# RWKV-7 group norm split into early and late columns with one variance row per head, gate and bonus computed earlier, state decay on VectorE and the sample state steps inside the solve levels

## The chip, the cores and the metric

The kernel runs on one core of one Trainium2 chip. The metric is the device time of one execution in microseconds (us). All arithmetic is float32. Besides TensorE (PE) with its weight load (PEld), the core has VectorE (DVE), ScalarE (ACT), GpSimd (POOL) and SyncE (SP), which issues most of the DMAs.

## The reference

One inference step of a two-layer decoder for 256 prompt tokens and 8 sample tokens (264 columns together). Each layer is a half-step FFN, a mixer (8 RWKV-7 heads beside 8 MLA heads), a cross-attention into 256 memory tokens, and a second half-step FFN. The change lies wholly in the mixer, and there in the RWKV half:

```
def step(S, inp):
    r_t, w_t, k_t, v_t, kk_t, b_t = inp
    S_kk = jnp.einsum('bhvk,bhk->bhv', S, kk_t)
    S = S * w_t[:, :, None, :] - S_kk[..., None] * b_t[:, :, None, :] + v_t[..., None] * k_t[:, :, None, :]
    return S, jnp.einsum('bhvk,bhk->bhv', S, r_t)
...
g = jax.nn.sigmoid(gd) @ g_up
mean = jnp.mean(o, axis=-1, keepdims=True)
var = jnp.mean(jnp.square(o - mean), axis=-1, keepdims=True)
o = ((o - mean) * lax.rsqrt(var + GN_EPS)).reshape(B, T, W) * gn_w + gn_b
bonus = jnp.sum(r_h * k_h * r_k, axis=-1, keepdims=True) * v_h
out = (o + bonus.reshape(B, T, W)) * g
...
x = x + jnp.concatenate([o_rwkv, o_mla], axis=-1) @ w_out[l]
```

The mean and the variance are taken per head and token over 64 values.

## The kernel before, in words

Activations lie transposed: features on the 128 partitions, the 264 tokens in the free dimension. Each engine has its own program, written by hand in the order in which it runs; a loop goes over the two layers. The engines meet through semaphores (`signal(name).by(...)` counts one up, `.at(k)` is the value that a wait wants). Every DVE and ACT instruction waits for the one before it on its engine.

The RWKV part of a layer stands between the MLA attention and the output projection, and has four stages.

1. **Operands** (`rwkv`, `solve` on PE). From the decays, four products per token are made: AR (kk and r), Bt, Kt, and their pairwise products MB and MK in 64-token chunks, two chunks (one pair `T`) to 128 partitions.
2. **Solve levels.** The inverse of a unit triangular 64x64 matrix per head and chunk is built in LEVELS = 6 doublings, so five rounds n = 1 to 5. In each round PE multiplies Y = Ml X for T = 0, 1, ACT copies Y out of PSUM, PE multiplies XT Y and Y XT, and DVE subtracts the results from X and XT (four 128x512 `TENSOR_TENSOR` a round; the last round has only the two of XT). GpSimd prepares the masks of the next rounds (`keep_level`, L509). `between(n)` puts further PE work between the two halves of a round. Behind the four subtractions DVE does one `step_samples(n - 1)` (a 128x2048 instruction of the 8 sample tokens' state update, nine of them numbered 0 to 8) and one `dcm` (the decay matrix of a chunk).
3. **Chunks** (`chunks` on PE). For the chunks n = 0 to 3 in turn: u = WT Z (64 rows, 4 products), DVE copies U out; PE adds into bank 6 the new keys (tok 2 times tok 3), the old state (identity times Z) and tok 1 times U, and DVE multiplies by the decay (`dcm[n]`) into Z[n + 1]. PE computes chunk n - 1's outputs before it waits for chunk n's U. Two `keep_warm` products (128x264, result unused) stand ahead of each wait for Z. DVE does `step_samples(5 to 8)` behind the first two U copies.
4. **Group norm, bonus, gate** (end of `rwkv` on PE and DVE). Over all 264 columns and 4 tiles: sums per head by the 128x128 matrix `blk`, subtraction of the mean, squares on ACT, sums of the squares (each on 64 partitions at once), a `RECIPROCAL` over 128x1056, a square root, and three further DVE instructions a tile, with the r k r_k product, the bonus and the gate in between.

Then `mix_out` multiplies by W_out in 8 column tiles, each in two halves of four products: half 0 takes the MLA rows, half 1 the RWKV rows. The first half of tiles 0 to 3 is issued as soon as the gate is out of PSUM; half 1 of each tile waits for `rwkv_mixed`. The weights come in 1 MB blocks of two tiles through a ring of two slots (`ring_c`): the block of tiles 4 and 5 is requested by SP when the two tiles of the first block are through. GpSimd's DMA queue loads the sample tokens' memory keys 4 to 7 (4 MB) after the last state and the last outputs, and the prompt memory (1 MB) after `rwkv_mixed`.

## Time and profile before

| | us |
|---|---|
| median of 3 runs (1904.67 to 1909.27) | 1905.67 |
| the profiled execution | 1913.24 |
| its span, first to last instruction | 1911.7 |
| PE busy | 1788.4 (94%) |
| PEld busy | 1483.9 (78%) |
| DVE busy | 638.0 (33%) |
| ACT busy | 315.1 (16%) |
| POOL busy | 84.5 (4%) |

The mean granted TensorE clock is 0.971 of full speed. One product in float32 stands as two instructions in the records, so a count of x32 is 16 products. Times in the traces are from the start of the span. The RWKV part of the first layer lies at 427 to 544 us, that of the second at 1363 to 1479 us.

### The profile page before, as it was taken

The numbers are of one execution on the slowest core, as the hardware profiler recorded it, in microseconds if no ns is written. First come the engines' busy times: TensorE is split into PE (matmuls) and PEld (weight loads), VectorE is DVE, ScalarE is ACT, GpSimd is POOL, SyncE is SP. The second block draws the span as 40 slices with busy tenths as digits, with TensorE's granted clock in tenths as the row PEclk, the third lists the DMA queues.
The fourth block names the chain that finished last, engine by engine and source line by source line (L and its number), as shares of the span: only waits on it lengthen the run. The fifth ranks groups of instructions, "written<-read, shape, count | busy, mean of one in ns | idle before, by whom it ended". The sixth has DMA issues, their size and how long they took to land.

```text
span 1911.7 us, 30695 instructions
## 1 busy us (share of the span) xinstructions
PE 1788.4 (94%) x11846; PEld 1483.9 (78%) x11846; DVE 638.0 (33%) x1250; ACT 315.1 (16%) x617; POOL 84.5 (4%) x99
## 2 busy tenths in 40 slices
PE   6999999878889999999999999997798999999995
PEld 5888887558767888888888888874686878888884
DVE  3111136548563321111121112546585612311122
ACT  1111002432100311110011100134221013111100
POOL 0000000014000000000000000000320000000000
PEclk9999999989899999999999999999799999999998
DMA  5444543841246634443434455346303474344431
GB/s 202 146 141 176 196 165 109 221 136 47 103 169 218 219 137 160 143 154 146 162 133 138 147 205 201 127 143 188 117 27 138 172 272 150 130 137 151 170 125 78
DMA packets 70641, 291.58 MB, mean 153 GB/s; under 512 B 8209, under 2 KB 41170, under 8 KB 41730
## 3 DMA queue, kind: packets, MB, share of 16 engines
q1 hardware_dynamic: 63938, 246.57, 37.7%
q0 software_dynamic: 6448, 42.20, 6.0%
q8 instruction: 70, 1.15, 0.3%
q10 hardware_dynamic: 144, 1.32, 0.2%
q14 instruction: 41, 0.34, 0.1%
HBM read 281.47 MB, written 8.59 MB: 152 GB/s over the span
## 4 chain that ended last, share of the span: by engine, by line
PE 86%; DVE 9%; ACT 2%; issue 2%; DMA 1%; DVEq 0%; SPq 0%; POOL 0%; ACTq 0%; POOLq 0%
PE bank L366 81%; DVE arena L1450 3%; PE bank L878 3%; PE bank L369 2%; ACT arena L1206 1%; DVE ring_a L1450 1%; DVE arena L1487 1%; DVE arena L1465 1%; DMA ring_c<-in_blocks 1%; DVE hT L1459 0%; DVE arena L1462 0%; DVE sq L1450 0%; DVE sq L1621 0%; DVE hT L1450 0%; DVE arena L1454 0%
## 5 line engine op out<-in xcount | busy, mean ns | idle before, releaser
L366 PE MATMUL bank<-hT,ring_a 128*128 128x264 f32 x2816 | 629.5, 387 | 18.9 <-DVEq L97 18.7
L366 PEld LDWEIGHTS bank<-hT,ring_a 128*128 128x128 f32 x2816 | 535.9, 190 | 111.1 <-issue 19.3
L366 PE MATMUL bank<-arena,ring_b 128*128 128x264 f32 x1408 | 314.3, 386 | 5.1 <-DVE arena L1514 5.1
L366 PEld LDWEIGHTS bank<-arena,ring_b 128*128 128x128 f32 x1408 | 267.2, 190 | 52.3 <-issue 6.8
L366 PE MATMUL bank<-arena 64*64 64x64 f32 (+6 forms) x3568 | 190.4, 273 | 20.8 <-DVE arena L1450 11.8
L366 PE MATMUL bank<-hT,ring_c 128*128 128x264 f32 x832 | 195.4, 393 | 12.5 <-DVE hT L1450 5.8
L366 PEld LDWEIGHTS bank<-hT,ring_c 128*128 128x128 f32 x832 | 158.8, 193 | 46.9 <-issue 8.4
L366 PEld LDWEIGHTS bank<-arena 64*64 64x64 f32 (+3 forms) x3568 | 149.1, 135 | 55.2 <-issue 44.4
L366 PE MATMUL bank<-arena,ring_c 128*128 128x264 f32 (+1 forms) x768 | 174.0, 385 | 1.3 <-ACT arena L1206 1.3
L366 PEld LDWEIGHTS bank<-arena,ring_c 128*128 128x128 f32 x768 | 144.9, 190 | 28.5 <-issue 5.0
L1206 ACT ACTIVATE arena<-bank 128x512 f32<-128x512 f32 (+5 forms) x220 | 95.4, 434 | 304.8 <-PE bank L366 255.6
L1514 DVE TENSOR_TENSOR arena<-arena,bank 128x264 f32 x88 | 37.8, 429 | 280.6 <-PE bank L366 276.3
L1510 DVE TENSOR_TENSOR arena<-bank,rstd 128x264 f32<-128x264 f32 x88 | 38.1, 433 | 247.6 <-PE bank L366 242.7
L1225 ACT ACTIVATE arena<-arena 128x264 f32<-128x264 f32 x88 | 37.2, 422 | 493.7 <-DVE arena L1510 493.7
L1459 DVE SCALAR_TENSOR_TENSOR sq<-bank,rstd 128x264 f32<-128x264 f32 x32 | 13.8, 433 | 253.7 <-PE bank L366 253.7
L1206 ACT ACTIVATE rstd<-rstd 128x264 f32<-128x264 f32 x9 | 3.8, 423 | 504.6 <-DVE rstd L1487 504.6
L366 PE MATMUL bank<-ring_c,arena 128*128 128x256 f32 (+2 forms) x472 | 72.5, 371 | 0.8 <-DVE arena L1462 0.8
L369 PE MATMUL bank<-con,arena 128*128 128x128 f32 (+1 forms) x284 | 43.7, 294 | 25.7 <-ACT arena L1206 25.7
L366 PEld LDWEIGHTS bank<-ring_c,arena 128*128 128x128 f32 (+1 forms) x472 | 55.5, 150 | 15.0 <-issue 8.2
L369 PEld LDWEIGHTS bank<-con,arena 128*128 128x128 f32 (+1 forms) x284 | 34.2, 148 | 35.1 <-issue 32.6
L878 PE MATMUL bank<-arena 64*64 64x64 f32 (+3 forms) x608 | 51.9, 268 | 6.7 <-DVE arena L1450 6.7
L1225 ACT ACT_TABLE_LOAD x44 | 56.5, 1283 | 1.7 <-ACT rstd L1206 1.0
(143 smaller groups left out, 1084.5 us busy)
## 6 DMA issues: line engine op xcount, KB each, us to landing
ring_a<-in_ffn_gu SPq DMA_DIRECT2D x88, 1024.0 KB, 4.8
ring_c<-in_blocks SPq DMA_DIRECT2D x58, 1024.0 KB, 4.9
ring_b<-in_ffn_down SPq DMA_DIRECT2D x32, 1408.0 KB, 6.2
arena<-in_pages SPq DMA_DIRECT2D x128, 144.0 KB, 2.5
arena<-in_mem_k POOLq DMA_DIRECT2D x8, 1024.0 KB, 7.8
arena<-in_mem_v POOLq DMA_DIRECT2D x8, 1024.0 KB, 7.2
ring_c<-in_pages SPq DMA_DIRECT2D x48, 144.0 KB, 2.5
ring_a<-in_pages SPq DMA_DIRECT2D x48, 144.0 KB, 2.4
```

Of the source, the lines that this page charges most:

```text
L366: return nc.tensor.matmul(out, lhsT, rhs, start=start, stop=stop)
L369: return nc.tensor.transpose(out, in_, ident[0:n, 0:n])
L878: return nc.tensor.matmul(out, lhsT, rhs, start=start, stop=stop, skip_group_check=True)
L1206: chain(nc.scalar.activation(out, in_, func, **more), signal(done) if done else None)
L1225: nc.scalar.activation(silu[:, u, :], silu[:, u, :], ACT.Silu), KF // 2)
L1450: chain(nc.vector.tensor_tensor(out, a, b, op), out_of(done))
L1459: chain(nc.vector.scalar_tensor_tensor(out=out, in0=a, scalar=s, in1=b, op0=op0, op1=op1), out_of(done))
L1465: chain(nc.vector.tensor_reduce(out, a, AX.X, ALU.max), out_of(done))
L1487: chain(nc.vector.reciprocal(ap, ap), signal("inverse_ready"))
L1510: nc.vector.tensor_tensor(silu[:, u, :], bank[u][:, 0:NT], rstd[:], ALU.mult), KF // 2)
L1514: nc.vector.tensor_tensor(hidden[:, 2 * i + u, :], silu[:, u, :], bank[2 + u][:, 0:NT], ALU.mult), KF // 2)
```

## The change

The order on DVE, in a layer's RWKV part, from the fourth solve round's last subtraction to the second chunk's U copy (register instructions left out). `bank` is PSUM; `ring_a<-...` 128x2048 are the sample steps, `arena<-con,arena` 128x512 is a `dcm`.

Before:

```order
L1450 TENSOR_TENSOR arena<-arena,bank5 128x512 [waits xt_ready,x_out]
L1450 TENSOR_TENSOR ring_a<-sq,ring_b 128x2048 [waits xt_out]
...
L1450 TENSOR_TENSOR arena<-con,arena 128x512 [waits dve_step]
...
L1450 TENSOR_TENSOR arena<-arena,bank2 128x512 [waits xt_ready,dve_step]
L1450 TENSOR_TENSOR arena<-arena,bank5 128x512 [waits xt_ready,xt_out]
L1450 TENSOR_TENSOR ring_a<-ring_a 128x2048 [waits xt_out]
...
L1462 COPY arena<-bank0 64x512 [waits wt_ready,dve_step]
L1450 TENSOR_TENSOR ring_a<-sq,ring_b 128x2048 [waits u_out]
...
L1450 TENSOR_TENSOR ring_a<-ring_a 128x2048 [waits dve_step]
...
L1450 TENSOR_TENSOR arena<-bank6,arena 128x512 [waits tok_turned,z_ready,vector_milestones]
L1462 COPY arena<-bank0 64x512 [waits u_ready,z_out]
```

The change:

```order
L1502 TENSOR_TENSOR ring_a<-ring_a 128x2048 [waits xt_out]
...
L1502 TENSOR_TENSOR ring_a<-ring_a,ring_b 128x2048 [waits vector_milestones]
...
L1502 TENSOR_TENSOR arena<-con,arena 128x512 [waits dve_step]
...
L1502 TENSOR_TENSOR small<-bank6,arena 128x264 [waits tensor_milestones,scalar_milestones]
...
L1511 SCALAR_TENSOR_TENSOR small<-small,vec,ring_b 128x264 [waits vector_milestones]
...
L1506 TENSOR_SCALAR ring_b<-ring_b,vec 128x264 [waits dve_step]
...
L1502 TENSOR_TENSOR arena<-arena,bank2 128x512 [waits xt_ready,dve_step]
L1502 TENSOR_TENSOR arena<-arena,bank5 128x512 [waits xt_ready,xt_out]
L1520 TENSOR_REDUCE sq<-ring_a 128x32 [waits xt_out]
...
L1514 COPY arena<-bank0 64x512 [waits wt_ready,dve_step]
L1502 TENSOR_TENSOR arena<-bank6,arena 128x512 [waits tok_turned,z_ready,u_out]
L1514 COPY arena<-bank0 64x512 [waits u_ready,z_out]
```

All nine steps now stand in the rounds (two in each of rounds 1 to 4, one in round 5), none between the chunks; rounds 4 and 5 also hold the bonus instructions (`small`, three a tile, two tiles a round; one tile stands here of each four).

On PE the second and third chunk. Before:

```order
L366 MATMUL bank<-con,ones 128x264 x2
L379 REGISTER_ALU [waits z_out]
L379 REGISTER_ALU [waits wt_out]
L878 MATMUL bank<-arena 64x128 x4
L878 MATMUL bank<-arena 128x128 x4
L878 MATMUL bank<-arena,con 128x128 x4
L878 MATMUL bank<-arena 64x64 x16
L379 REGISTER_ALU [waits u_out]
L878 MATMUL bank<-arena 128x128 x4
```

The change:

```order
L380 REGISTER_ALU [waits z_out]
L380 REGISTER_ALU [waits wt_out]
L859 MATMUL bank<-arena 64x128 x4
L859 MATMUL bank<-arena 128x128 x4
L380 REGISTER_ALU [waits u_out]
L859 MATMUL bank<-arena 128x128 x4
L859 MATMUL bank<-arena 128x64 x4
L859 MATMUL bank<-arena 64x64 x16
```

The two unused products and the identity product are gone, and a chunk's outputs (128x64 and 64x64) stand behind its own state product instead of ahead of it.

The rest of the change in the code: the tiles' places; the gate product on PE in the attention, in place of four unused products; the bonus products in `between`; PE behind the chunk loop, whose body for n < 3 now issues keys, state and outputs of its own chunk; and DVE's rounds and chunks.

```diff
+EARLY = 3 * CHUNK
-        r = Region(arena, MIX, ARENA)
-        gate = r.take(NJ, NT)
-        bonus = r.take(NJ, NT)
-        e1 = r.take(NJ, NT)
-        e2 = r.take(NJ, NT)
+        gate, bonus = w1, small[:, 0:NJ * NT].rearrange("p (j t) -> p j t", j=NJ)
+        r8 = wstat[0:H, :]
...
-                keep_warm(4, 6)
+                pe.wait_ge(*signal("prob_t_out").at(units))
+                pe.wait_ge(*signal("olat_out").at(units))
+                pe.wait_ge(*signal("gd_ready").at(1))
+                for j in range(NJ):
+                    last = mm(bank[2 * j + 1 if j < 3 else 6][:, 0:NT], sw("g_up")[:, j * P:j * P + P], p[:, 13, :])
+                signal("gate_up").by(last)
...
                 def between(n):
+                    if n >= 4:
+                        wait_apart(pe, signal("rkr_ready").at(1))
+                        for i in range(2):
+                            if n == 5:
+                                wait_apart(pe, signal("bonus_out").at(i + 1))
+                            else:
+                                wait_apart(pe, signal("tok_out").at(9 + i))
+                            signal("bonus_ready").by(mm(bank[6 + i][:, 0:NT], c("blk"), bonus[:, 2 * (n - 4) + i, :]))
...
+                wait_apart(pe, signal("rwkv_out").at(3))
+                centred(False)
+                wait_apart(pe, signal("so_loaded").at(1))
...
+                wait_apart(pe, signal("u_out").at(4))
                 outputs(3)
+                variance(False)
+                wait_apart(pe, signal("rwkv_out").at(4))
+                wait_apart(pe, signal("so_out").at(1))
+                centred(True)
+                new_keys(3)
+                wait_apart(pe, signal("gn_scaled").at(1))
+                variance(True)
+                state(3)
+                spread(False)
+                spread(True)
...
-                    step_samples(n - 1)
+                    for i in range(2 * n - 2, min(2 * n, 9)):
+                        step_samples(i)
...
+                    if n >= 4:
+                        bonuses(n)
...
-                    if n < 2:
-                        step_samples(5 + 2 * n)
-                        step_samples(6 + 2 * n)
+                    if n:
+                        tt(Zd, Z[n], flat(dcm[n]), ALU.mult)
+                    if n == 3:
+                        group_norm()
...
-                    tt(Z[n + 1], bank[6][:, 0:512], flat(dcm[n]), ALU.mult, "z_out")
+                    tt(Z[n + 1], bank[6][:, 0:512], flat(dcm[n]), ALU.mult, None if n else "z_out")
+                    if n:
+                        tt(Z[n + 1], Z[n + 1], Zd, ALU.add, "z_out")
```

`centred` multiplies by one constant matrix that subtracts the head's mean (identity minus 1/64 in the head's block); `variance` sums the squares with an 8-column matrix, one row per head; `spread` brings the eight rows of inverse roots back to 128 partitions. Each runs once for the early columns (0 to 191, chunks 0 to 2) and once for the late (192 to 263). DVE's `group_norm` (behind the fourth U copy) copies the sample outputs, scales the centred values by the gate times gn_w, and takes the reciprocals on 8x192 and 8x72; ACT takes squares (2 of 128x384, 1 of 128x288) and the roots. After the last state DVE multiplies by the spread roots and adds the bonus: two 128x384 products and one 128x768 sum for the early columns, one product and one sum of 128x288 for the late. The bonus tile is now (bonus + gn_b) times the gate. The product r k r_k moves to the end of the attention on DVE; the gate's sigmoid on ACT moves to the projections, its four copies to the time before the MLA outputs, and the sqrt table is asked for ahead of the chunk outputs. In `mix_out`, tile 2 waits for the last state and tile 3 for the early half of `rwkv_mixed`, since the spread roots lie in their banks. The constants grow by 672 columns (344 KB).

## Rows read from the trace of the kernel before

**Rows 1.** Page, part 4: the chain that ended last, by engine.
```profile
PE 86%; DVE 9%; ACT 2%; issue 2%; DMA 1%; DVEq 0%; SPq 0%; POOL 0%; ACTq 0%; POOLq 0%
```
**Rows 2.** Windows, first layer: span, then busy of PE, PEld, DVE, ACT, POOL, clock, DMA.
```profile
451.71:459.41 7.70, 7.70 (x238) 7.46 (x236) 6.67 (x6) 2.40 (x4) 3.91 (x2) 1.00 0.02 4
459.41:465.94 6.53, 6.53 (x230) 6.53 (x228) 5.73 (x6) 2.39 (x4) 3.61 (x3) 1.00 0.01 3
...
473.53:480.91 7.38, 6.10 (x187) 5.83 (x185) 7.10 (x9) 1.19 (x2) 1.09 (x1) 1.00 0.01 2
480.91:489.29 8.38, 5.78 (x137) 4.97 (x133) 8.24 (x5) 1.54 (x4) 0.05 (x1) 1.00 0.02 4
489.29:500.25 10.96, 10.73 (x66) 9.54 (x67) 5.97 (x5) 0.38 (x1) 1.11 (x2) 0.50 0.42 153
500.25:509.30 9.05, 9.05 (x79) 7.47 (x78) 1.37 (x2) 0.38 (x1) 0.53 (x1) 0.85 0.41 168
509.30:516.60 7.30, 7.30 (x82) 6.55 (x80) 1.37 (x2) 0.38 (x1) 0.00 (x0) 1.00 0.01 2
516.60:543.93 27.33, 20.22 (x114) 14.89 (x113) 20.56 (x32) 7.51 (x12) 2.71 (x5) 1.00 0.41 164
543.93:548.20 4.27, 4.27 (x12) 3.42 (x13) 1.93 (x5) 0.00 (x0) 0.53 (x1) 0.60 0.59 182
```
**Rows 3.** Timeline of DVE in rounds 1 and 2: start, duration, engine, line, operation.
```profile
455.41 2.29 DVE L1450 TENSOR_TENSOR ring_a<-ring_a,ring_b 128x2048 f32<-128x2048 f32 x1 [0.22 <-DVE arena L1450]
457.74 1.64 DVE L1450 TENSOR_TENSOR arena<-con,arena 128x512 f32<-128x512 f32 x1
459.41 2.85 DVE L1450 TENSOR_TENSOR arena<-arena,bank 128x512 f32<-128x512 f32 x4
462.30 2.29 DVE L1468 TENSOR_REDUCE sq<-ring_a 128x32 f32<-128x2048 f32 x1
```
**Rows 4.** Timeline of POOL in the same rounds.
```profile
455.50 5.02 POOL L509 TENSOR_TENSOR arena<-arena,con 128x512 f32<-128x512 f32 x2 [4.27 <-PE bank L366]
462.26 2.51 POOL L509 TENSOR_TENSOR arena<-arena,con 128x512 f32<-128x512 f32 x2 [1.75 <-PE bank L366]
```
**Rows 5.** Timeline of PE in the chunks, at the low clock and at the full one.
```profile
489.52 3.94 PE L878 MATMUL bank<-arena 128*64 128x128 f32 x16 [2.03 <-DVE arena L1450]
...
499.35 2.13 PE L366 MATMUL bank<-con,ones 128*128 128x264 f32 x4
...
509.51 2.17 PE L878 MATMUL bank<-arena 128*64 128x128 f32 x16
...
512.60 5.38 PE L878 MATMUL bank<-arena 128*128 128x64 f32 x88
```
**Rows 6.** Timeline of POOL, ACT, DVE and PE in the last chunks and the norm.
```profile
503.41 0.53 POOL L527 DMA_DIRECT2D sq<-sample_outputs  x1 [5.37 <-DMA sample_outputs<-sq]
...
524.68 1.08 ACT L1206 ACTIVATE arena<-hT 128x1056 f32<-128x1056 f32 x1 [4.49 <-PE bank L366]
...
529.84 6.75 DVE L1487 RECIPROCAL arena<-arena 128x1056 f32<-128x1056 f32 x1
...
531.54 7.38 PE L366 MATMUL bank<-hT,ring_c 128*128 128x264 f32 x32 [1.82 <-ACT arena L1206]
```
**Rows 7.** The chain that ended last, at the output projection: start, duration, what.
```profile
543.93 4.19 PE bank L366 x10
...
548.28 4.70 DMA ring_c<-in_blocks
...
553.01 12.06 PE bank L366 x53
```
**Rows 8.** Page, part 6: DMA issues, size of one, median us to landing.
```profile
ring_c<-in_blocks SPq DMA_DIRECT2D x58, 1024.0 KB, 4.9
...
arena<-in_mem_k POOLq DMA_DIRECT2D x8, 1024.0 KB, 7.8
```
**Rows 9.** Timeline of DVE at the start of the RWKV part.
```profile
427.19 1.42 DVE L1450 TENSOR_TENSOR arena<-ring_b 128x512 f32<-128x512 f32 x2 [4.48 <-ACT hT L1206]
```

231 lines of the change are left out of this document (139 added, 92 removed).

## The prediction, made before the changed kernel ran

> **What bounds the kernel now.** I read the page first, then the chain that ended last, then windows over the RWKV part, then timelines. The chain gives PE 86% of the span and DVE 9% [rows 1]: nearly everywhere PE works without a stop, and time can only be won where it doesn't. The change touches one such place in each layer. In the windows of the first layer [rows 2] I cut it at its hand-overs. Solve rounds 1 and 2 take 7.70 and 6.53 us with PE busy throughout. From 473.53 us on DVE is the full engine (7.10 of 7.38, then 8.24 of 8.38 us) until the first chunk state is out at 489.29. Then three chunk rounds of 10.96, 9.05 and 7.30 us go on the path PE to DVE and back, the first at clock 0.50. The group norm takes 27.33 us until PE runs freely at 543.93. The second layer runs the same program with the same buffers, so I work out one layer and double it.
>
> I measure a layer from 451.71 (first subtraction of round 1) to 553.01, where the output projection's third weight block has landed [rows 7]; behind that nothing changes.
>
> **Stretch one: rounds and sample steps (451.71 to 489.29, 37.6 us).** The change takes nothing off DVE's total here; it packs it. Steps cost 2.29 us each [rows 3], the four subtractions 2.85 us together, a `dcm` 0.70 us when alone. Two steps and a `dcm` make a round of DVE work of 2.85 + 4.64 + 0.72 = 8.2 us, while PE needs 6.5 to 7.7 us for a round [rows 2]. So DVE becomes the bound of rounds 1 to 4. In round 1 DVE also waits for PE between its subtractions as now (0.9 us): 9.2 us.
>
> There is a tax. The `dcm` at 457.74 took 1.64 us, not 0.70, and POOL's two masks took 5.02 us beside DVE's 2.29 us step, but 2.51 us beside the reduction at 462.30 [rows 3, 4]. DVE instructions with two SBUF operands and POOL's masks exclude each other; PSUM operands and reductions don't suffer. The Trainium skill ("SBUF — State Buffer", SBUF: two separate sides) says the same: the port pair is an exclusive lock held for the whole instruction, with two SBUF inputs on VectorE among the cases. With that rule the trace agrees: 5.02 against 2.51 us. In rounds 2 and 3 two such steps stand where one mask after the other arrives, and I charge two waits totalling 1.6 us each (from 1.64 - 0.70 = 0.94 us, to 2.51 us when both masks block): 9.8 us each. Bounds: 8.2 and 10.7.
>
> Round 4 gets two steps and the bonus: 8.66 us until the first bonus product is out, 1.35 us to the second (three 128x264 instructions of 0.45; 512 columns take 2.85 / 4 = 0.71 [rows 3]). Round 5's PE work waits in `between(5)` for this second tile. Behind it stand 0.44 us of bonus product, then XT products of 0.95 us and a hand-over of 0.25: 12.2 us from round 4 to round 5's first subtraction, against 5.9 now. Then both subtractions (2.1 with PE's second product), the last step 2.3, two more bonus tiles 2.7, U copy 0.7, and state, hand-over and Z 2.4: 10.2 us.
>
> Sum: 9.2 + 9.8 + 9.8 + 12.2 + 10.2 = 51.2 us, **13.6 us more** than now. Bounds +10 and +17. PE idles for some 5 us ahead of `between(5)`.
>
> **Stretch two: chunks, norm, projection (489.29 to 553.01, 63.7 us).** Count from Z of chunk 0 (T). Price of PE at the full clock: 16 records of 128x128 in 2.17 us less the tail, so 0.9 us for each of u, keys and state; 88 records of which 80 are two chunks' outputs in 5.38 us, so 2.2 us for outputs [rows 5]. A chunk round becomes: u 0.9, hand-over 0.25, U copy 0.69, hand-over 0.2 (keys hidden in these), state 0.9, outputs 2.2 = 5.2 us. DVE's two new instructions (decay and sum, 0.7 each) and Z 0.7 lie beside U's wait and the outputs: 0.25 + 0.7 + 0.7 = 1.65 us after the state, under 2.2. So the decay costs nothing while outputs cover it, 0.7 us a round if they didn't. Against 10.96, 9.05 and 7.30 the rounds lose the identity product (0.9), two unused products (1.1) and outputs ahead of the state (2.2).
>
> Then, in PE's order and with N = 264 at 7.38 / 32 = 0.23 us a record [rows 6], so 0.17 for 192 columns and 0.06 for 72: u of chunk 3 ends at T + 11.3; early centring 1.3, sample transposes 0.4, outputs 2.2, early variance 1.3 end at 16.5; late centring 0.5, keys 0.9, late variance 0.5, state 0.9 end at 19.3; spreads 1.3 and 0.5 end at 21.1. Off PE: the reciprocal went from 6.75 us for 1056 columns to 6.4 ns a column: 1.3 us for 192, 0.5 for 72, and the early root is out at 18.9, ahead of the state's end. ACT squares are 0.5 us pieces (1.08 for 1056 columns [rows 6]). DVE: last Z 21.1, early half out 23.2, late half 24.1. The projection's first halves (16 products, 32 records, 7.1 us) start at 21.1 and end at 28.2; tile 3 needs the early half at 26.4, so nothing waits. Two tiles of second halves (3.5 us at full clock, where now ten records took 4.19 us at 0.60 [rows 2, 7]) free the block at T + 31.7. Now the same point is 548.14, T + 58.9.
>
> The block then took 4.70 us to land [rows 7]. With the change POOL's 4 MB of memory keys start at T + 25 and are still moving, so I take 6.0 us, between 4.7 and 7.8 (the keys' own median, against 4.9 for blocks) [rows 8]. Landed: T + 37.8, against T + 63.7: **25.9 us less**.
>
> **The clock.** Now it sinks to 1.2 GHz in both layers as soon as PE has idled 2 us ahead of the first chunk, and returns only around the unused products at 499.35 us [rows 5], although PE was busy all that time [rows 2]. These products go. I charge one chunk round at the low level: u, keys (now longer than the cover), state and outputs 8.6 instead of 5.2, **3.4 us**. Bounds: 0 and 18 (below). The Trainium skill ("TensorE: Matmul & The Clock Gate", Why this matters for your kernels) advises keeping idle gaps between bursts of products short lest the clock halve; the change opens a gap of about 5 us in round 5. [...]
>
> **Edits at nothing.** Gate product: four 128x264 products for four unused ones of that size, behind the same wait; its ACT copies end before the MLA outputs need ACT. r k r_k (2.9 us on DVE) fits the 4.48 us in which DVE waits for the MLA copies [rows 9]; without that cover it costs 2.9. Sigmoid and table load on ACT: idle there. The sample outputs' two DMAs start at T - 5.8, the first is waited for 5.4 us [rows 6], so both take some 12; PE wants them at T + 12.6. The constants' extra 344 KB land in the first FFN.
>
> **Sum.** Per layer 13.6 - 25.9 + 3.4 = -8.9 us; two layers -17.8. From the profiled 1913.24 us this is 1895.4; the median stands 7.6 us below the profiled execution, so **1888 us**.
>
> **Rivals.**
> - *R1, clock low through all chunk rounds* until the centring. Rounds 8.6, 8.6, plus first outputs and last u: 11.5 us instead of 3.4 a layer. For it: nothing of full width is left in the rounds. Against: the remaining products are denser. Gives -0.8 a layer, 1904 us: no change.
> - *R2, slower: the low clock lasts into the projection.* Centring, variance, outputs, keys, state and spreads at half speed add up to 6.5 us more, partly beside DVE, so 18 a layer: +5.7 a layer, **1917 us**; without the key loads in the way (-1.3), 1914. It decides from 12.3 us of clock loss a layer on.
> - *R3, rounds cheaper than I think*: masks slip beside reductions, the bonus wait is short: +10 in place of +13.6, clock high throughout: -15.9 a layer, 1874 us.
> - *R4, the won time is given back at the block*: loads of memory keys and prompt memory hold it to 7.8 us or more: 2 to 4 us a layer, 1892 to 1896.
>
> **How the numbers follow.** Forecast with R4, 1880 to 1897: 0.50. R3: 0.16. R1: 0.19. R2: 0.15. About 0.3% (6 us) is what a measurement can tell from no change. Faster than 1900: forecast, R3 and a small part of R1, 0.69. Within 0.3%: most of R1, 0.16. Slower: most of R2, 0.15. The range reaches from R3's 1873 to 1910, which leaves out R2.
>
> **What would show it.** Right: DVE without idle from round 1's last subtraction to round 4's bonus, rounds of 9 to 10 us; the first Z some 51 us after round 1's first subtraction; chunk rounds near 5.2 us where the clock is 1.00; the first projection product at T + 21; no `RECIPROCAL` over 1.5 us in the norm. Wrong: clock 0.50 over the whole chunk stretch (R1, R2), or PE waiting inside the norm for a root or for the sample outputs, or for a block over 6 us.

## The result, and the profile after

| | before | after |
|---|---|---|
| median, 4 runs each (us) | 1906.18 (1904.67 to 1909.27) | 1928.31 (1926.45 to 1933.41) |
| the profiled execution (us) | 1913.24 | 1928.28 |
| its span (us) | 1911.7 | 1926.7 |
| mean granted TensorE clock | 0.971 | 0.956 |

The ratio of after to before is 1.0132 (in brackets, here and below, its 95% interval: [1.0099, 1.0164]). The change makes the kernel slower, by 22 us as the difference of the medians and by 25 us as the ratio has it, where the prediction said 18 us faster. The chain that ended last has the same shares as before, so it tells nothing (part 4 of the page of after; answers to [rows 1]):

```profile
PE 86%; DVE 9%; issue 2%; ACT 1%; DMA 1%; DVEq 0%; SPq 0%; POOL 0%; ACTq 0%; POOLq 0%
```

The windows of the first layer do (after; columns as in [rows 2]: span, busy of PE, PEld, DVE, ACT, POOL, clock, DMA share, GB/s):

```profile
448.32:457.41 9.09, 9.09 (x287) 8.86 (x284) 8.03 (x8) 2.39 (x4) 4.57 (x2) 1.00 0.02 4
457.41:466.99 9.58, 8.26 (x270) 7.91 (x264) 9.34 (x7) 2.39 (x4) 4.37 (x2) 1.00 0.01 3
466.99:476.58 9.59, 7.26 (x196) 6.57 (x196) 9.35 (x7) 1.20 (x2) 4.38 (x2) 1.00 0.02 3
476.58:490.20 13.62, 7.58 (x107) 5.95 (x108) 10.60 (x13) 1.20 (x2) 0.61 (x1) 0.58 0.20 79
490.20:500.68 10.48, 8.02 (x189) 7.52 (x189) 7.60 (x11) 3.02 (x6) 0.55 (x1) 0.83 0.42 155
500.68:508.98 8.30, 8.30 (x54) 7.63 (x51) 2.77 (x4) 0.38 (x1) 0.54 (x1) 0.50 0.16 65
508.98:518.44 9.46, 9.46 (x66) 8.67 (x65) 2.76 (x4) 0.38 (x1) 0.00 (x0) 0.50 0.00 0
518.44:539.07 20.63, 20.63 (x151) 17.12 (x150) 7.67 (x14) 2.99 (x8) 0.00 (x0) 0.64 0.00 1
```

The first five rows are the five solve rounds and the first chunk up to its Z: 52.4 us, where 51.2 were forecast. Rounds 2 and 3 are full of DVE (9.34 of 9.58). Then everything is PE, busy without a stop, at clock 0.50, half of full speed: a chunk round takes 9.46 us and not 5.2.

The tax on steps beside masks is there too. Timeline of DVE and of POOL in round 2 of after (answers to [rows 3, 4]):

```profile
460.29 2.66 DVE L1502 TENSOR_TENSOR ring_a<-ring_a,ring_b 128x2048 f32<-128x2048 f32 x1
462.99 3.25 DVE L1502 TENSOR_TENSOR ring_a<-sq,ring_b 128x2048 f32<-128x2048 f32 x1
...
460.98 3.10 POOL L510 TENSOR_TENSOR arena<-arena,con 128x512 f32<-128x512 f32 x1 [0.17 <-PE bank L367]
```

The steps take 2.66 and 3.25 us instead of 2.29, 1.3 us together where the prediction charged 1.6.

Timeline of PE in round 5 and the first chunk (the bracket is idle time ahead, and what ended it):

```profile
477.40 1.15 PE L367 MATMUL bank<-arena 64*64 64x64 f32 x32 [2.03 <-DVE arena L1502]
478.84 1.98 PE L367 MATMUL bank<-arena 64*64 64x64 f32 x32 [0.30 <-DVE arena L1502]
485.57 1.22 PE L367 MATMUL bank<-small,con 128*128 128x264 f32 x2 [4.75 <-DVE small L1502]
...
496.91 1.13 PE L859 MATMUL bank<-arena 64*128 64x128 f32 x8 [1.95 <-DVE small L1502]
498.54 21.74 PE L859 MATMUL bank<-arena 64*128 64x128 f32 x159 [0.51 <-DVE arena L1514]
```

PE idles twice for the bonus: 4.75 us ahead of `between(5)`'s first product, which was foreseen, and 1.95 us (2.32 us in layer 2) in front of the first chunk, which the prediction did not name: the keys of chunk 0 go into bank 6, and so wait for the last bonus tile. Ahead of both it stops for 2.03 us, for the subtractions of round 4. Finer windows show what the clock does around these three (same columns, after):

```profile
474.00:478.00 4.00, 1.97 (x68) 1.86 (x65) 3.89 (x4) 0.00 (x0) 0.00 (x0) 1.00 0.02 4
...
478.00:480.00 2.00, 1.70 (x41) 1.59 (x38) 1.90 (x3) 0.60 (x1) 0.00 (x0) 0.70 0.00 0
480.00:482.00 2.00, 0.82 (x16) 0.63 (x12) 1.97 (x2) 0.60 (x1) 0.00 (x0) 0.50 0.00 0
...
485.50:492.00 6.50, 6.25 (x76) 4.89 (x78) 2.89 (x7) 0.00 (x0) 0.00 (x0) 0.50 0.11 43
492.00:494.80 2.80, 2.80 (x125) 2.80 (x122) 2.77 (x2) 0.77 (x2) 0.00 (x0) 0.92 0.03 6
494.80:498.50 3.70, 1.28 (x18) 0.98 (x10) 3.37 (x8) 2.25 (x4) 0.55 (x1) 1.00 0.57 184
498.50:500.00 1.50, 1.46 (x12) 1.26 (x13) 0.01 (x1) 0.00 (x0) 0.00 (x0) 0.77 1.02 428
500.00:526.00 26.00, 26.00 (x181) 23.51 (x180) 7.59 (x11) 1.59 (x4) 0.54 (x1) 0.50 0.08 33
```

The clock falls from 2.4 GHz (1.00) to 1.2 GHz (0.50) at 478.8, between the stop of 2.03 us and that of 4.75 us, so it is low already when the long one begins. It comes back behind products in a row (from 492). It falls again at 499.3, 2.4 us after PE has begun chunk 0's keys, and stays low until 533.4, for 34 us, although PE never stops.

The norm itself does what was said: no reciprocal over 1.34 us, and nothing waits for a root (DVE timeline of after; [rows 6] had 6.75 us):

```profile
533.05 1.34 DVE L1800 RECIPROCAL arena<-arena 8x192 f32<-8x192 f32 x1
...
536.08 0.59 DVE L1806 RECIPROCAL arena<-arena 8x72 f32<-8x72 f32 x1
```

The last loss is at the projection (chain of after; answers to [rows 7]):

```profile
551.87 9.31 DMA ring_c<-in_blocks
...
561.23 13.93 PE bank L367 x55
```

The block takes 9.31 us instead of 4.70. Each layer, from the first subtraction of round 1 to the end of that wait, in the profiled executions:

| layer | before | predicted | after | first Z out | then to the block's request | landing |
|---|---|---|---|---|---|---|
| 1 | 101.3 | 92.4 | 112.9 | 52.4 | 51.2 | 9.3 |
| 2 | 101.4 | 92.4 | 109.9 | 53.1 | 47.4 | 9.4 |

Together these two stretches take 20.1 us more than before. The two profiled executions as wholes differ by only 15.0 us, so that outside the stretches the profiled execution of after was 5 us shorter. No run shows why; before_bare below, whose code is that of before up to the chunks, also reached its first subtraction 3.6 us earlier than before did, so scatter alone can be of this size. In the second layer the first Z to projection stretch was 3.7 us shorter, with the same rounds of 9.46 us: the clock came back 2.5 us after the first centring product, in the first layer only 10.9 us after it.

### The profile page after: what moved, and what is told of

Its sections match the earlier page's. It is cut to its first block, busy times and chain, and to the rows that moved or that the text cites. A ratio compares the mean times of both kernels' runs of the same rounds, so it can differ in the third digit from the quotient of the medians.

```text
span 1926.7 us, 30701 instructions
## 1 busy us (share of the span) xinstructions
PE 1792.2 (93%) x11814; PEld 1493.5 (78%) x11814; DVE 636.9 (33%) x1260; ACT 312.3 (16%) x621; POOL 86.5 (4%) x99
## 4 chain that ended last, share of the span: by engine, by line
PE 86%; DVE 9%; issue 2%; ACT 1%; DMA 1%; DVEq 0%; SPq 0%; POOL 0%; ACTq 0%; POOLq 0%
PE bank L367 81%; DVE arena L1502 3%; PE bank L859 3%; DVE ring_a L1502 2%; PE bank L370 2%; ACT arena L1250 1%; DMA ring_c<-in_blocks 1%; DVE arena L1517 1%; DVE sq L1520 0%; DVE sq L1502 0%; DVE arena L1514 0%; DVE sq L1673 0%; DMA page_table<-in_page_table 0%; DVE ring_b L1679 0%; PE bank L847 0%
## 5 line engine op out<-in xcount | busy, mean ns | idle before, releaser
L367 PE MATMUL bank<-hT,ring_a 128*128 128x264 f32 x2816 | 629.7, 387 | 18.1 <-DVEq L98 18.1
L367 PEld LDWEIGHTS bank<-arena 64*64 64x64 f32 (+3 forms) x3568 | 153.2, 139 | 63.9 <-issue 53.6
L1250 ACT ACTIVATE arena<-bank 128x512 f32<-128x512 f32 (+7 forms) x218 | 95.0, 436 | 331.4 <-PE bank L367 283.3
L1566 DVE TENSOR_TENSOR arena<-arena,bank 128x264 f32 x88 | 37.8, 430 | 280.3 <-PE bank L367 276.1
L1511 DVE SCALAR_TENSOR_TENSOR sq<-bank,rstd 128x264 f32<-128x264 f32 x32 | 13.9, 433 | 253.7 <-PE bank L367 253.7
L859 PE MATMUL bank<-arena 64*64 64x64 f32 (+3 forms) x608 | 66.8, 319 | 5.3 <-DVE small L1502 4.3
L859 PEld LDWEIGHTS bank<-arena 64*64 64x64 f32 (+3 forms) x608 | 60.4, 216 | 10.3 <-issue 8.5
L1502 DVE TENSOR_TENSOR xT<-xT,bank 128x264 f32<-128x264 f32 x32 | 13.7, 429 | 153.6 <-PE bank L367 153.3
```

The lines of the kernel that those rows point to most:

```text
L367: return nc.tensor.matmul(out, lhsT, rhs, start=start, stop=stop)
L859: return nc.tensor.matmul(out, lhsT, rhs, start=start, stop=stop, skip_group_check=True)
L1250: chain(nc.scalar.activation(out, in_, func, **more), signal(done) if done else None)
L1502: chain(nc.vector.tensor_tensor(out, a, b, op), out_of(done))
L1511: chain(nc.vector.scalar_tensor_tensor(out=out, in0=a, scalar=s, in1=b, op0=op0, op1=op1), out_of(done))
L1566: nc.vector.tensor_tensor(hidden[:, 2 * i + u, :], silu[:, u, :], bank[2 + u][:, 0:NT], ALU.mult), KF // 2)
```

## The experiments

The kernels of a set share their runs of the kernel before; its medians were 1901.6 (13 runs), 1903.95 (19), 1904.0 (13) and 1903.5 us (19) in the four sets below, and single runs went from 1892 to 1914. The profiled execution of before that the prediction started from, 1913.24 us, is near the slow end of these. Kernels are compared by their ratio to before. "Round" is U copy to U copy, for chunks 1, 2 and 3.

### First set: clock, queue, packing

**warm**: the unused products put back, two ahead of each wait for Z.

```diff
                     if n:
+                        keep_warm(2)
                         wait_apart(pe, signal("z_out").at(n))
```

> The changed kernel with the two unused 128x264 products back ahead of each wait for Z in chunks 1 to 3. Theory 1 (clock): the chunk stage is slow because TensorE sits at 1.2 GHz from before the first Z until the centring, and the full-width products are what lifts it. Then the clock is 1.00 from about the second chunk on, a round falls from 9.4 us to about 6.5 (5.2 plus the two products), the first projection product comes at Z1 + 26 to 31 us instead of Z1 + 38.4, and the kernel gains 14 to 24 us: 1904 to 1914. Theory 1b (order): the rounds are slow because a chunk's outputs stand between its state and the next u, and the low clock is only a companion. Then two more products a round make it 2 us a round slower: about 1938.

Measured: 1918.05 us, ratio 1.0093 [1.0058, 1.0127]. Its profiled execution was the quickest of its seven, 1906.83. There the rounds are 8.36, 6.32 and 6.31 us in the first layer instead of 6.12, 9.46 and 9.46, and first Z to projection 29.5 instead of 38.4 us. The other theory, that the order makes the rounds slow, falls. Windows of warm, columns as above:

```profile
493.00:497.00 4.00, 1.17 (x10) 0.99 (x9) 3.62 (x8) 2.25 (x4) 0.55 (x1) 0.99 0.58 188
497.00:503.00 6.00, 6.00 (x45) 4.77 (x45) 0.69 (x1) 0.38 (x1) 0.53 (x1) 0.50 0.55 229
504.50:510.80 6.30, 6.30 (x69) 5.45 (x69) 2.77 (x4) 0.38 (x1) 0.00 (x0) 1.00 0.01 3
```

So two wide products a round bring the clock back within one round, in both layers, and pay for themselves, 8.9 us in the first layer and 5.2 in the second; but the fall behind the idle stretch is still there. The gain fell short of the 14 to 24 us expected: by the ratios it is some 7 us, and the intervals of warm and of the changed kernel overlap. Every single run of warm was below every one of the changed kernel, but in that set the kernel before, too, ran 5 us quicker.

**keys**: the four memory keys are held until the projection's fifth tile is through.

```diff
                 wait_apart(pool, signal("rwkv_ready").at(4))
+                wait_apart(pool, signal("mix_ready").at(5))
```

> The changed kernel, with GpSimd's loads of memory keys 4 to 7 held until five tiles of the projection are through. Theory 2 (queue): the projection's third block takes 9.3 us instead of 4.7 because 5 MB of keys and prompt memory are in flight when it is asked for. Then it lands 4.7 to 5.5 us after its request, and the kernel gains about 4 us a layer: 1920. Its rival: the block's delay has another cause (the request waits in SP's queue); then it stays at 9 us and the time at 1928. A third case: the keys come too late for the cross-attention, and PE waits there for them; then some of the gain is lost and shows as waits for mem_k.

Measured: 1926.25 us, 1.0133 [1.0096, 1.0169], as the changed kernel. The chain of keys says why:

```profile
549.20 4.81 DMA ring_c<-in_blocks
...
561.61 9.92 DMA ring_c<-in_blocks
```

The third block is quick, the next one takes the place of it behind the same 4 MB. The wait had only moved.

**steps**: the sample steps back where they were before, one a round, and 5 to 8 behind the first two U copies.

```diff
-                    for i in range(2 * n - 2, min(2 * n, 9)):
-                        step_samples(i)
+                    step_samples(n - 1)
...
+                    if n < 2:
+                        step_samples(5 + 2 * n)
+                        step_samples(6 + 2 * n)
```

> The changed kernel with the sample steps where they were before: one in each solve round, two behind each of the first two U copies. Theory 3 (packing): the rounds are bound by DVE work since two steps stand in each. Then the stretch from round 1's first subtraction to round 4's falls from 28.3 us to about 22, the U copy comes some 7 us earlier, and 4.6 us come back ahead of the first Z: net 3 to 5 us a layer, 1919 to 1922. Rival: the steps cost the same anywhere, since the first Z waits for the sum of DVE's work; then only the two steps behind the second U copy (4.6 us) leave the path, and POOL's exclusion too. If PE idles less in the rounds the clock may also stay high, which would give up to 17 us a layer more and would show in the granted clock, not in the rounds.

Measured: 1915.01 us, 1.0058 [1.0031, 1.0085]. First Z after 46.1 us (52.4), in the second layer 46.0 (53.1). First Z to projection is 37.8 and 34.4 us, as in after (38.4 and 34.7): the sample outputs come in time from there too. So packing all steps in the rounds costs 6 to 7 us a layer and buys nothing behind them, as long as the clock is low there. At the full clock no run shows it: VectorE's 2.76 us of a chunk round and two steps of 2.29 us make 7.3 us, an estimate from these rows, which is more than the 5.2 us of such a round.

**warm_keys**: both of the first two edits.

> Both of the first two edits. If they are independent (theories 1 and 2), the gains add: 1896 to 1906. If the held keys matter only while the chunk stage is slow, or more when it is fast (the requests come closer together then), the sum differs by some us, and the time from the block's request to its landing tells which.

Measured: 1914.15 us, 1.0068 [1.0038, 1.0098]. Chunk rounds nearly as in warm (8.87, 6.66 and 6.31 us in the first layer), block waits as in keys (4.67, then 9.84 us). The expected 1896 to 1906 us supposed that both edits gain; keys gains nothing.

### Second set: paced loads, the decay, the bonus out of the rounds

**paced**: prompt memory first, then the keys one at a time.

```diff
+                wait_apart(pool, signal("rwkv_mixed").at(2))
+                signal("mem_loaded").by(pool.dma_start(memg, t["mem"]))
                 for b in range(4, NS):
+                    wait_apart(pool, signal(("mix_ready", "mix_ready", "mq_ready", "mq_ready")[b - 4]).at((5, 7, 1, 3)[b - 4]))
...
-                wait_apart(pool, signal("rwkv_mixed").at(2))
-                signal("mem_loaded").by(pool.dma_start(memg, t["mem"]))
```

> Edit: in the changed kernel the prompt memory is asked for first and the memory keys 4 to 7 one by one, behind mix_ready 5, mix_ready 7, mq_ready 1 and mq_ready 3. Theory (the weight blocks wait because 4 MB of keys are in flight at once on the other queue): the third block lands 4.7 to 5.5 us behind its request in place of 9.3, no later block over 6 us, PE goes on 4 us earlier in each layer and keeps it: 8 to 9 us less than the changed kernel, ratio to before near 1.009, and the sample scores of keys 4 to 7 wait for nothing. Rival (the bytes must move anyway and the wait only shifts, as it did when all four were held back together): the third block is quick, a later block or key takes over 9 us and PE waits for it; time as the changed kernel within 3 us.

Measured: 1917.27 us, 1.0073 [1.0047, 1.0099]; block landed after 4.74 us in both layers, and the chain has no other block in it up to the end of the projection:

```profile
548.73 4.74 DMA ring_c<-in_blocks
...
553.51 18.51 PE bank L367 x82
```

What holds a block is how much is in flight beside it, not that the bytes have to come.

**decay_pe**: the state decay of chunks 1 to 3 back on PE.

```diff
+                    if n:
+                        for j in range(NJ):
+                            add(bank[6][:, js], ident, Z[n][:, js])
...
-                        tt(Zd, Z[n], flat(dcm[n]), ALU.mult)
...
-                        tt(Z[n + 1], Z[n + 1], Zd, ALU.add, "z_out")
```

> Edit: only the decay goes back to PE (identity times Z added in bank 6 in chunks 1 to 3; the two extra VectorE instructions of each chunk go). Theory (clock low, PE is the bound of a chunk round): the identity product is 8 records of 128x128, 1.97 us at the low clock by the timeline of before (3.94 us for 16), and nothing on VectorE gets shorter that PE waits for, so U copy to U copy goes from 9.46 to about 11.4 us in the two full rounds, and the stretch from the first Z to the projection grows by 5 to 6 us a layer: about 1.0055 times the changed kernel, 1939 us where it is 1928. Rival (the clock stays low because nothing of the full 128 rows and columns is left between the chunks): the identity product is full width, the clock comes back in the second or third round, rounds of 6 to 8 us, the stretch gets 3 to 8 us shorter a layer: 1912 to 1922 us.

Measured: 1933.65 us, 1.0159 [1.0109, 1.0209]. Rounds 6.81, 11.76, 11.76:

```profile
502.86:514.62 11.76, 11.76 (x73) 10.52 (x74) 1.39 (x2) 0.38 (x1) 0.00 (x0) 0.50 0.01 1
```

2.3 us a round at the low clock. The rival falls: four products of 128 rows and 128 columns a round did not bring the clock back.

**late_bonus**: one bonus product in round 5 and one behind each of the first three state products, all through bank 7; DVE does tile 0 behind the first U copy and tiles 1 to 3 behind Z. The wait of chunk 0 for the last tile is gone.

```diff
-                    if n >= 4:
-                        ...
+                    if n == 5:
+                        bonus_product(0)
...
-                    else:
-                        wait_apart(pe, signal("bonus_out").at(4))
...
                         state(n)
+                        bonus_product(n + 1)
...
-                    if n >= 4:
-                        bonuses(n)
...
+                    if n == 0:
+                        bonus_tile(0)
...
+                    if n < 3:
+                        bonus_tile(n + 1)
```

> Edit: in the changed kernel the four bonus products and their twelve VectorE instructions leave rounds 4 and 5; one product stands in round 5 and one behind each of the first three state products, and VectorE does a tile behind the first U copy and behind each of the first three Z. Theory (packing: the bonus costs 8 us in the rounds, and VectorE has 3 us to spare in each chunk round): first subtraction of round 1 to first Z goes from 52.4 to 44 to 45 us, U copy to U copy from 9.46 to about 10.3 us at the low clock (one full-width product of 0.9 us more), together 6 us less a layer, ratio to before near 1.007. If the clock comes back in the chunks, because PE idles less in front of them or has a full-width product in each, rounds of 6 us: another 8 us less a layer, ratio near 0.998. Rival (the bonus instructions delay the next U copy): rounds over 11 us, no gain.

Measured: 1888.77 us, 0.9925 [0.9902, 0.9947]: 40 us below the changed kernel, and better than the ratio near 0.998 that was expected with the clock back. That it is the 1888 us which the prediction had said of the changed kernel is coincidence. First Z after 43.2 us (52.4 and 53.1 in after), rounds 4.94, 5.69 and 5.66, first Z to projection 24.7 and 25.6 us (38.4 and 34.7). Over both layers of the profiled executions the solve rounds are 19 us shorter and the stretch behind them 23 us. Clock (windows of late_bonus):

```profile
480.00:486.00 6.00, 5.71 (x111) 4.80 (x112) 5.86 (x5) 1.20 (x2) 0.61 (x1) 0.72 0.03 7
486.00:488.50 2.50, 0.99 (x34) 0.89 (x32) 2.40 (x4) 0.00 (x0) 0.00 (x0) 1.00 0.97 383
488.50:494.15 5.65, 5.65 (x155) 5.12 (x151) 5.28 (x7) 3.02 (x6) 0.55 (x1) 1.00 0.33 107
498.88:504.55 5.67, 5.67 (x69) 5.18 (x67) 4.04 (x8) 0.38 (x1) 0.00 (x0) 1.00 0.00 0
```

Ahead of the chunks it falls once, in round 5, and is back before them. There is no idle time between the last solve product and the first keys. PE does stop 3 us earlier, for 1.51 us and in layer 2 for 2.01 us, and the clock stays at 1.00.

**late_bonus_warm_paced**: that, with `keep_warm(1)` ahead of each of those bonus products, and the loads paced.

> Edit: the bonus moved as in late_bonus, one unused 128x264 product ahead of each of those bonus products, and the loads paced as in paced. If the three losses (clock, packing, queue) are separate and add: first subtraction to first Z 44 to 45 us, chunk rounds 6.3 us, first Z to first projection product 29.5 us, block request 13.7 us later, 4.8 us to land: 93 us against 101.3 of before and 112.9 of the changed kernel in layer 1, so 16 us less than before over two layers, ratio near 0.992 to 0.995. Rival (they do not add: VectorE becomes the bound in the chunks or the sample outputs are waited for when the chunks are short): rounds near 7.5 us or a wait for the outputs of the samples of 3 us and more, ratio 0.998 to 1.003.

Measured: 1877.52 us, 0.9864 [0.9815, 0.9913]. From the first subtraction to the end of the block wait 88.5 and 85.1 us (before: 101.3 and 101.4). By the ratios paced gains 0.0059 on the changed kernel and this one 0.0061 on late_bonus: the gains of bonus and queue add.

### Third set: what keeps the clock up?

late_bonus had changed two things that might hold the clock: no idle time in front of the chunks (theory A), and a wide product in each of the first three (theory B).

**gap_fill**: seven unused products in the 4.75 us.

```diff
                             if n == 5:
+                                if i == 0:
+                                    keep_warm(7, 1)
                                 wait_apart(pe, signal("bonus_out").at(i + 1))
```

> Edit: the changed kernel, with seven unused 128x264 products (3.1 us at the full clock) in PE's idle time of 4.75 us ahead of the first bonus product of round 5; the chunks stay as they are, without any full-width product. It tells which of two things late_bonus owed its high clock to. Theory A (the idle time ahead of the chunks starts the low clock): it stays at 1.00, U copy to U copy 5.2 to 5.7 us in place of 9.46, first Z to first projection product about 25 us; 11 to 13 us less a layer than the changed kernel, ratio to before near 1.000. Theory B (the low clock needs wide products in the chunks to come back, whatever came before): the clock is low by the second chunk, rounds of 9.46 us again, time within 4 us of the changed kernel, ratio 1.011 to 1.014.

Measured: 1924.88 us, 1.0103 [1.0039, 1.0168]. The first idle time is down to 0.72 us. The clock falls ahead of it as in after, is back behind the unused products and 1.00 from 487 to 494.7 us; but the second, 2.10 us, is still there, and the clock falls behind it. Rounds 6.81, 9.46, 9.46 again. It did not tell A from B, since only one of two gaps was filled.

**one_wide**: one unused product behind each of the first three state products.

```diff
                         state(n)
+                        keep_warm(1)
```

> Edit: the changed kernel with one unused 128x264 product behind each of the first three state products, where late_bonus has its bonus product; the bonus itself and PE's idle time of 4.75 us stay in rounds 4 and 5. Theory B (a wide product in each chunk is what matters): clock 1.00 by the second or third round, rounds of 5.7 us there, 8 to 10 us less a layer than the changed kernel, ratio near 1.004. Theory A (the idle time matters, and one wide product in a round does not bring the clock back): rounds of 10.3 us, 2 us more a layer, ratio near 1.014.

Measured: 1931.91 us, 1.0157 [1.0097, 1.0218]; rounds 7.99, 10.34, 10.34 at 0.50:

```profile
504.91:515.25 10.34, 10.34 (x67) 9.34 (x68) 2.77 (x5) 0.38 (x1) 0.00 (x0) 0.50 0.01 2
```

One wide product of each round is pure cost once the clock is low; two (warm) bring it back. The two also stand at another place, ahead of the wait for Z, so number and place are not told apart.

**late_bonus_paced**: late_bonus and paced, no unused product.

> Edit: late_bonus with the loads paced as in paced, and without the unused products of late_bonus_warm_paced. If the clock of late_bonus holds (rounds 4.94, 5.69, 5.66 us) and the block lands in 4.8 us: 1.3 us less a layer than late_bonus_warm_paced, about 1875 us, ratio near 0.985. If the clock was luck and the unused product is needed: rounds of 9 to 10 us in one layer or both, 1885 us and more.

Measured: 1876.59 us, 0.9868 [0.9809, 0.9927]; rounds 4.94, 5.68, 5.67 in both layers, block landed in 4.64 and 4.84 us. Each round is 0.45 us shorter than in late_bonus_warm_paced, which the medians cannot tell apart.

**late_bonus_decay_pe**: late_bonus with the edit of decay_pe.

> Edit: late_bonus with the decay back on PE as in decay_pe. It prices the decay at the full clock. The recorded count says that VectorE's two added instructions cost nothing and the identity product 0.9 us a round; of that the wait for the U copy covers some: keys and identity take 1.8 us against 1.14 us of hand-overs and copy. Expected 0.7 to 0.9 us more in each of the two full rounds and in the last chunk, 2 to 2.7 us a layer, 1893 to 1894 us where late_bonus has 1889, ratio near 0.995. Rival (VectorE has become the bound of the round, 2.8 us of chunk work and 1.3 us of bonus): no change or a gain.

Measured: 1890.41 us, 0.9939 [0.9910, 0.9968]; the intervals overlap. In the trace a round goes from 5.68 to 6.88 us, and first Z to projection from 24.7 and 25.6 to 28.2 and 28.3:

```profile
502.85:509.73 6.88, 6.88 (x75) 6.15 (x76) 2.66 (x5) 0.38 (x1) 0.00 (x0) 1.00 0.00 0
```

The decay on VectorE is worth 1.2 us a round at the full clock, some 3 us a layer by the trace, of which the first layer's block takes one back (landed after 8.48 us in late_bonus, 7.46 here). The medians are only 1.6 us apart and cannot tell it from nothing.

### Fourth set: the clock from both sides, and DVE in the rounds

**both_gaps**: gap_fill, and the second gap filled.

```diff
                     else:
+                        wait_apart(pe, signal("wt_out").at(1))
+                        keep_warm(4, 2)
                         wait_apart(pe, signal("bonus_out").at(4))
```

> Edit: gap_fill, and four more unused products (1.8 us at the full clock) in the second idle time, the 2.10 us in which PE waits for the last bonus tile ahead of the first chunk; still nothing of 264 columns in the chunks. Theory A (idle time ahead of the chunks makes the clock fall, and the narrow products do not bring it back): clock 1.00 in the chunks, rounds of 5.2 to 5.7 us, first Z to first projection product about 25 us, ratio to before near 1.000. Theory B (the narrow products of the chunks pull it down by themselves, and a wide one in each round is needed to hold it): rounds of 9.46 us again, ratio near 1.010.

Measured: 1904.53 us, 1.0008 [0.9975, 1.0041], single runs 1898 to 1916. The profiled execution shows both theories' pictures, one in each layer (windows of both_gaps, layer 1 above, layer 2 below):

```profile
495.60:498.00 2.40, 1.86 (x14) 1.73 (x15) 1.47 (x3) 0.34 (x2) 0.00 (x0) 1.00 0.90 379
498.00:500.00 2.00, 2.00 (x39) 1.81 (x38) 0.69 (x1) 0.38 (x1) 0.00 (x0) 0.88 1.01 422
500.00:510.00 10.00, 10.00 (x69) 9.21 (x68) 2.77 (x4) 0.38 (x1) 0.53 (x1) 0.50 0.07 26
...
1433.50:1436.00 2.50, 1.87 (x15) 1.73 (x15) 1.53 (x3) 0.45 (x2) 0.00 (x0) 1.00 0.91 357
1438.00:1449.00 11.00, 11.00 (x134) 9.96 (x132) 5.52 (x8) 0.77 (x2) 0.53 (x1) 1.00 0.07 25
```

In layer 2 the clock stays at 1.00 through the chunks without one wide product in them, rounds of 5.24 us (the forecast's 5.2), first Z to projection 23.3 us. So in this layer the narrow products did not pull it down, and no wide one was needed to hold it: B falls as it was stated. In layer 1 it fell all the same, 2.2 us after PE had gone on behind the short stop of 0.51 us for the U copy, which is in both layers; rounds 9.46. Filling the gaps does not exclude the fall. That it makes it rarer rests on one layer of two here, against none of the 19 named at the end.

**late_bonus_idle**: late_bonus, with a stop in front of the chunks put in.

```diff
+                        if n == 0:
+                            wait_apart(pe, signal("tile_done").at(1))
                         new_keys(n)
...
-                        ts(gate[:, j, :], gate[:, j, :], v("gn_w", j), ALU.mult)
+                        ts(..., done="tile_done" if j == 0 else None)
```

> Edit: late_bonus with a wait more: PE starts the first chunk's keys only when VectorE has the whole first bonus tile, so that PE idles for 2.3 us in front of the chunks, as in the changed kernel; the bonus products stay in the chunks. Theory A (idle time): clock 0.50 from the first or second round, rounds of 10 us, first Z to first projection product 33 to 38 us, 8 to 12 us more a layer than late_bonus, ratio 1.001 to 1.006. Theory B (a wide product in each chunk holds it up): clock 1.00, only the first Z comes 1.3 to 2 us later, ratio 0.994 to 0.996.

Measured: 1917.93 us, 1.0074 [1.0047, 1.0101]: by the ratios 28 us slower than late_bonus for a wait that moves the first Z by 2.2 to 2.5 us. Windows of late_bonus_idle:

```profile
1424.00:1428.00 4.00, 1.71 (x35) 1.60 (x28) 2.23 (x5) 2.25 (x4) 0.55 (x1) 1.00 0.61 193
1428.00:1430.00 2.00, 2.00 (x9) 1.20 (x7) 0.69 (x1) 0.00 (x0) 0.00 (x0) 0.56 1.00 418
1430.00:1432.00 2.00, 2.00 (x33) 1.84 (x32) 1.28 (x3) 0.00 (x0) 0.53 (x1) 0.50 0.63 262
```

These windows are from layer 2: PE stops for 2.29 us in front of the keys, and 1.6 us after it has begun again the clock falls, with the wide products in place. Rounds 9.83, 10.34, 10.34, and 9.34, 10.34, 10.34 in layer 1, where the stop in front of the keys was only 0.74 us, behind one of 3.02 us in round 5. The time is a little over the range of theory A (1.001 to 1.006), its picture is A's: A holds, and a wide product in each round does not hold the clock up.

**before_bare**: the kernel before, without its two unused products in each chunk.

```diff
                     if n:
-                        keep_warm(2)
                         wait_apart(pe, signal("z_out").at(n))
```

> Edit: the kernel before without the two unused products ahead of each wait for Z; everything else as it was. If they brought the clock back (the recorded prediction charged their loss with 3.4 us a layer, and up to 18): second and third round go from 11.8 and 7.3 us to 10 to 13 us at the low clock, 5 to 9 us more a layer, ratio 1.005 to 1.010. If the dense 128-row identity products bring it back without them: rounds of 6.3 us, 2 to 3 us less a layer, ratio near 0.997.

Measured: 1931.47 us, 1.0140 [1.0077, 1.0202]. Rounds 8.32, 10.93 and 12.53 us:

```profile
499.15:511.68 12.53, 11.50 (x73) 10.45 (x74) 1.38 (x3) 0.39 (x1) 0.53 (x1) 0.50 0.12 47
511.68:541.25 29.57, 26.21 (x145) 21.74 (x145) 11.15 (x21) 5.24 (x10) 2.69 (x5) 0.63 0.39 151
```

The clock falls at 485.5 us, in a stop for the first Z as in before (there at 489.3), and is low until 533.3, where before had it back at 503.0. A layer takes 114.7 us instead of 101.3. The ratio is over the range expected (1.005 to 1.010). The six unused products of a layer, which the change deletes, are worth 13.4 us a layer in the order of before, more than the change lost.

**late_bonus_paced_dcm**: late_bonus_paced, with the decay matrices made by ACT.

```diff
-                        tt(dcm[n - 1], over(c("blk"), P, NJ, P), din[...].broadcast_to([P, NJ, P]), ALU.mult)
...
+                        for j in range(NJ):
+                            run(dcm[n - 1][:, j, :], c("blk"), scale=din[:, j, CHUNK * n - 1:CHUNK * n], ...)
```

> Edit: late_bonus_paced with the four decay matrices (dcm, one 128x512 product of VectorE in each of rounds 1 to 4) made by ScalarE instead, four 128x128 copies with a scale per partition each. It tests the packing term: if VectorE is the bound of the rounds, each round gets 0.7 us shorter, those in which dcm waited for a GpSimd mask 0.9 to 1.6 us: first subtraction to first Z from 43.2 to 39 to 40.5 us, 5 to 8 us less in all than late_bonus_paced, 1869 to 1872 us. Rival (the steps then wait for the masks instead, or ScalarE delays its copies of Y): first Z less than 1 us earlier, no difference.

Measured: 1872.26 us (1863.53 to 1875.28), 0.9835 [0.9774, 0.9897]. The profiled execution is the quickest of the four. First Z after 40.4 us instead of 43.2 in both layers. Windows of rounds 1 to 3, first subtraction to first subtraction:

```profile
446.53:454.88 8.35, 8.35 (x261) 8.12 (x258) 7.32 (x6) 5.48 (x12) 4.56 (x2) 1.00 0.02 4
454.88:463.83 8.95, 8.73 (x294) 8.54 (x290) 8.74 (x7) 4.04 (x9) 4.47 (x3) 1.00 0.01 4
463.83:472.69 8.86, 6.28 (x195) 5.91 (x192) 8.65 (x7) 2.80 (x6) 4.38 (x2) 1.00 0.01 3
```

Each of the first three is some 0.7 us shorter than in late_bonus_paced (9.08, 9.60 and 9.60 us): DVE bounds these rounds. In this execution the clock stays at 1.00 through the rounds, although PE stops for 2.34 and 2.29 us behind the subtractions of rounds 4 and 5. This is the quickest version of the study; its interval overlaps that of late_bonus_paced, so that the last step is seen in the trace rather than in the times.

## Why the prediction was wrong

- **Where the kernel is bound, stretch one.** Right: 52.4 and 53.1 us against 51.2. DVE was the bound of rounds 1 to 4, the tax of masks beside steps was 1.3 us for the 1.6 charged, the idle time ahead of `between(5)` 4.75 us for "some 5". The Trainium skill ("SBUF — State Buffer", SBUF: two separate sides), which the prediction drew on, has the same lock; the trace agrees with 2.66 and 3.25 us beside masks against 2.29 us alone.
- **Stretch two at the full clock.** Nearly right in its mechanism: layer 2 of both_gaps, the one stretch of the changed order that ran at 1.00 throughout, had rounds of 5.24 us for 5.2. It reached the projection's first product after 23.3 us for 21.1 and the block's request after 34.4 for 31.7, so norm and projection were 2.7 us too short in the sum.
- **The clock: the step that failed.** "I charge one chunk round at the low level: 3.4 us" with "Bounds: 0 and 18". That the clock falls at the chunks was read rightly: the kernel before stops for 2.03 us for its first Z, in front of the second chunk [rows 5], and its clock falls there in both layers. The changed kernel has such a stop in front of the first chunk instead, 1.95 and 2.32 us, since chunk 0 waits for the last bonus tile. Wrong was that the clock comes back by itself after one round. The prediction had read that it returned around the unused products at 499.35 [rows 5] (at 503.0, 1.5 us behind them), though PE had been busy nearly all along, and it knew that the change deletes these. In after the clock was low for 34 us in layer 1 and 27 in layer 2. The block's request came 19.5 us (layer 1) and 15.7 us (layer 2) later than the forecast without the clock; less the 2.7 us above, the low clock cost 16.8 and 13.0 us where 3.4 were charged. Half of the time at 0.50 from the first Z to the request, 18.1 and 13.9 us, an estimate from the windows, says nearly the same.
- **What shows it.** before_bare deletes the unused products alone: 48 us at the low clock instead of 14, and 13.4 us a layer. Put back into the changed order (warm) they bring the clock back in the first round, but return only some 7 us in all by the ratios; the stop and the packed rounds are still in it. late_bonus takes the stop in front of the keys away, and the clock holds without any unused product; late_bonus_idle puts a stop in again, and it falls. The Trainium skill ("TensorE: Matmul & The Clock Gate", Why this matters for your kernels) advises short idle gaps between bursts of products; late_bonus_idle agrees, at 14 us a layer for 2.2 us of delay; the page warns of longer gaps than the 2.29 us that were enough here, and the measurement decides. The prediction looked at the gap of 5 us in round 5 as what might lower the clock; it was low already when that gap began, and 1.00 again ahead of the chunks.
- **The block (R4).** Its mechanism was right, its size too small: 9.3 us for 6.0, that is 3.3 us a layer, and over the 7.8 us that R4 names. paced shows that it could have been had for nothing.
- **The decay on VectorE.** Right that it costs nothing where PE is busy: DVE has 2.76 us of work in a round of 9.46. It saves 1.2 us a round at the full clock and 2.3 at the low one, against 0.9 in the prediction's count and 1.97 in what was expected of decay_pe.
- **Edits at nothing.** From the first chunk to the projection's block PE waits for neither the roots nor the sample outputs, as forecast. The moved gate product, r k r_k and sigmoid were not tested by themselves; after reaches its first subtraction at 448.32 us, before at 451.71, so no cost beyond the scatter named above shows.
- **The rivals.** R1 had the clock return with the centring, which is about layer 2. In layer 1 it returned 6 us before the projection, which is nearly R2, though not into the projection. R2's time, 1914 to 1917 us, was still too low, by the block, the norm and the rounds. R3 did not happen.

The sum by layer 1: 51.2 + 1.2, then 31.7 + 2.7 + 16.8, then 6.0 + 3.3 make 112.9 us. The clock's term alone, in two layers, is 29.8 us where 6.8 were charged. Small slips in the prediction's text change nothing: R3 comes to 1874 us and the range says 1873.

What stays open: why, with both gaps filled, the clock fell in one layer and not in the other. In all 19 profiled layers in which PE stopped for 1.95 to 2.33 us directly in front of chunk 0's keys (after, warm, keys, steps, warm_keys, paced, decay_pe, gap_fill and one_wide, and layer 2 of late_bonus_idle) the clock fell within 2.5 us of their start. In none of the ten without a stop there (late_bonus and the four kernels built on it without that wait) did it fall in the chunks. The length of a stop alone does not decide: stops of 2.0 to 2.5 us elsewhere in the rounds passed without a fall, and layer 1 of late_bonus_idle fell with 0.74 us in front of the keys. The runs also show that rounds of narrow products can go by at 1.00 when the clock is up (both_gaps, layer 2) and do not raise it when it is down, and that one wide product a round did not raise it either, but two did. They do not show what decides at a stop of 0.5 us.

## What to carry to other kernels

- Before an edit deletes products whose result nobody uses, run one kernel with only these deleted: here they were worth 13 us a layer in the order they were made for, more than the whole change lost, and less in the new order. And look at the granted clock in windows of a few us, with the idle time ahead of each fall; a mean over the span (0.971 to 0.956) hides it.
- When work of another engine is to be packed under a busy PE, put it where that engine has time left in each round (here the chunk rounds), and never so that PE stops in front of a stretch of small products. Moving the bonus from one to the other, with not an instruction less, was worth 40 us, about half of it through the clock.
- Large loads that nobody needs soon go out one at a time. Held back together they only move the wait.

## What was not expected of the hardware

- PE at clock 0.50 for 34 us while busy without a stop, in the first 23 us with products of 64 and 128 rows and 64 and 128 columns; the same products at 1.00 in layer 2 of both_gaps. Two unused 128x264 products a round brought the clock back within one round, one (at another place in the round) did not, nor did four identity products of 128x128.
- A 1 MB block asked for while 4 to 5 MB of another queue are in flight took 9.3 us, against 4.7 when those were paced. Holding four loads back for one block gave the same wait, 9.9 us, to the next.
- ACT makes a decay matrix in four copies of 128x128 with a scale per partition in 1.70 us, for 0.69 us on DVE, and the GpSimd masks beside it took no longer (4.56 against 4.57 us in round 1).
